# A hybrid layer in fp32 on one core: expert outputs are turned back during the last expert rounds, and the weight ring waits for the first gathered rows

## What is computed

```
def hier_moe(h2, ...):
    ...
    tok = zeros(n_rows).at[dest].set(flat_t[order])       # assignments sorted by expert
    ...
    def expert_block(args):
        xb, e = args
        hid = silu(xb @ w_gate_e[e]) * (xb @ w_up_e[e])
        return hid @ w_down_e[e]
    ys = lax.map(expert_block, (xs, block_e))
    return zeros_like(h2).at[tok].add(ys * wt[:, None])    # weighted sum back to the tokens

x = x + y_moe                                              # end of the first block
hn = rmsnorm([meta, x], a_norm_g);  qkv = hn @ a_w_qkv     # start of the second
```

## Time and profile before

| what | us |
|---|---|
| median of three runs | 2805.41 |
| lowest and highest run | 2804.01, 2805.78 |
| profiled execution, its own time | 2804.31 |
| its span from the first to the last instruction | 2802.5 |
| first ring load issued | 790.07 |
| gather 0 issued | 810.37 |
| first expert product starts | 823.41 |
| last "up" product starts | 1296.45 |
| last write of YSO ends | 1309.88 |
| first product of the combine | 1314.24 |
| first and second weights of the second block, first products | 1351.23 and 1360.02 |
| sums of the squares on PE | 1367.46 |

### The profile page before, as it was taken

The page is one execution under the profiler, slowest core; times in us unless marked ns, Lnnn a source line. Parts: engine busy times, 40 slices in busy tenths (PEclk is TensorE's granted clock), DMA queues, the critical chain, the costliest instruction groups (busy, mean ns, idle before and its releaser), DMA issues.

```text
span 2802.5 us, 41956 instructions
## 1 busy us (share of the span) xinstructions
PE 2608.5 (93%) x16786; PEld 2134.3 (76%) x16786; DVE 1150.9 (41%) x2012; ACT 1032.6 (37%) x2128; POOL 837.9 (30%) x532
## 2 busy tenths in 40 slices
PE   8999899999978888888999989999999999999999
PEld 6877788888855555455887769999998887777877
DVE  7754676231241111111356552232446776512212
ACT  4444444432222211112355544322324555532231
POOL 1002565223311223100221006645531110465553
PEclk9999999999989999999999989999999999999999
DMA  4330111433359999996211102323322111233332
GB/s 145 83 78 23 31 39 39 113 85 96 87 220 394 426 426 426 426 425 252 68 52 59 50 24 75 99 81 88 100 80 61 46 46 39 60 90 91 105 92 67
DMA packets 311731, 370.43 MB, mean 132 GB/s; under 512 B 10208, under 2 KB 283744, under 8 KB 286960
## 3 DMA queue, kind: packets, MB, share of 16 engines
q1 hardware_dynamic: 310384, 363.52, 37.2%
q0 software_dynamic: 1152, 4.19, 0.4%
HBM read 363.49 MB, written 4.19 MB: 131 GB/s over the span
## 4 chain that ended last, share of the span: by engine, by line
PE 67%; DMA 12%; DVE 9%; ACT 5%; POOL 3%; issue 3%; ACTq 0%; SPq 0%; DVEq 0%; POOLq 0%
DMA early<-in_w_up_e 11%; PE bank L2300 5%; PE bank L1823 5%; PE bank L2301 4%; PE bank L2302 4%; PE bank L2793 4%; PE bank L2794 4%; PE bank L2795 4%; PE bank L442 4%; PE bank L444 4%; PE bank L443 4%; POOL split L2275 2%; DVE early L683 2%; PE bank L3055 1%; PE bank L1060 1%
## 5 line engine op out<-in xcount | busy, mean ns | idle before, releaser
L2275 POOL TENSOR_TENSOR split<-keep,split 128x1024 fp32r<-128x1024 f32 x143 | 351.5, 2462 | 460.8 <-ACT split L2249 460.8
L2300 PE MATMUL bank<-x_hi,split 128*128 128x264 f32 (+1 forms) x1280 | 400.5, 313 | 21.9 <-POOL split L2275 9.4
L2301 PE MATMUL bank<-x_lo,split 128*128 128x264 f32 (+1 forms) x1280 | 392.7, 307 | 0.0
L2302 PE MATMUL bank<-x_hi,split 128*128 128x264 f32 (+1 forms) x1280 | 392.4, 307 | 0.0
L2249 ACT ACTIVATE split<-keep 128x1024 fp32r<-128x1024 f32 x192 | 200.2, 1049 | 222.1 <-PE bank L2795 208.0
L2300 PEld LDWEIGHTS bank<-x_hi,split 128*128 128x128 f32 x1280 | 243.7, 190 | 44.0 <-issue 20.8
L1823 PE MATMUL bank<-early 128*64 128x256 f32 x2048 | 236.0, 383 | 43.3 <-DMA early<-in_w_up_e 35.8
L1823 PEld LDWEIGHTS bank<-early 128*64 128x64 f32 x2048 | 166.4, 138 | 124.3 <-issue 79.3
L2301 PEld LDWEIGHTS bank<-x_lo,split 128*128 128x128 f32 x1280 | 244.0, 191 | 10.0 <-issue 0.2
L2302 PEld LDWEIGHTS bank<-x_hi,split 128*128 128x128 f32 x1280 | 242.8, 190 | 10.4
L2831 DVE TENSOR_TENSOR mlp<-mlp,bank 128x264 f32<-128x264 f32 (+1 forms) x96 | 49.5, 516 | 326.6 <-ACT mlp L2810 326.6
(11 more groups left out here) (476 smaller groups left out, 6089.5 us busy)
## 6 DMA issues: line engine op xcount, KB each, us to landing
early<-in_w_gate_e SPq DMA_DIRECT2D x64, 1024.0 KB, 11.1
early<-in_w_up_e SPq DMA_DIRECT2D x64, 1024.0 KB, 11.8
early<-in_w_down_e SPq DMA_DIRECT2D x64, 1024.0 KB, 11.3
early<-in_w_in SPq DMA_DIRECT2D x68, 512.0 KB, 3.7
keep<-in_mlp_w_in SPq DMA_DIRECT2D x64, 512.0 KB, 3.9
keep<-in_mlp_w_out SPq DMA_DIRECT2D x64, 512.0 KB, 3.9
keep<-in_a_w_qkv SPq DMA_DIRECT2D x24, 512.0 KB, 3.7
early<-in_w_ssd_out SPq DMA_DIRECT2D x16, 512.0 KB, 3.9
```

What stands on the lines that cost most here:

```text
L2275: e.tensor_tensor(lo, x, whole(hi), ALU.subtract).then_inc(*u.free(sig_, "lo", n))
L2300: e.matmul(o, hi[:, k, :], xh, start=k == 0, stop=False, skip_group_check=True)
L2301: e.matmul(o, hi[:, k, :], xl, start=False, stop=False, skip_group_check=True)
L2302: m = e.matmul(o, lo[:, k, :], xh, start=False, stop=k == 7, skip_group_check=True)
```

## The change

Five things are changed.

1. **Ring.** After the four stores of `h_rows`, SP waits until gather 0 has landed before it issues the next ring loads.
2. **Arrival.** ACT now copies the first bank of a gather, DVE the second.
3. **Window.** DVE reads both starts of a pair's window before it waits for the gathered rows.
4. **Rows turned back early.** "turn" s for s = 0 to 5 stands at the end of rounds 27 to 32, and "turn" 6 at the start of round 33. Each turns both halves of block s; ACT copies each bank once, with the weight, to YK, which lies over YSO. "half" 0 to 2 (rounds 27 to 29) and 3, 4 (round 33) make the upper and lower halves of q = 0 from YK in SBUF. YKL lies over YK too. Only block 7 is still turned in the combine.
5. **Combine.** PE starts with s = 0 to 4, turns block 7, and does s = 5 to 7. For tiles t = 4 to 7 the order is t outermost: one bank gets all eight blocks and is then done. PE and DVE no longer wait for the last write of YSO before they read the count. The function table load and the masks on ACT stand behind the halves. The third keep load of the second block waits for PE's s = 1.

The diff, cut (the wide path gets the same steps in its own branch, which is not taken):

```diff
-        def arrive_dve(e, n):
+        def arrive_act(e, n):
             b = BR.of("gather", n, 0)
             e.wait_ge(*GA.pe.to(n, 0))
...
+            if r == 33:
+                EXPERT += [("turn", 6), ("half", 3), ("half", 4)]
...
+            if 27 <= r < 33:
+                EXPERT.append(("turn", r - 27))
+            if 27 <= r < 30:
+                EXPERT.append(("half", r - 27))
...
                         e.dma_start(hrows[128 * c:128 * c + 128, :], HS[:, c, :]).then_inc(*d_rows.land(c))
+                    e.wait_ge(*d_got[0].to(0))
...
+        def return_pe(e, s_):
+            for q in range(2):
+                b = XR.take("yk", s_, q)
+                for s, n in b.before:
+                    e.wait_ge(s, n)
+                e.wait_ge(*F.act.to("y", 2 * (24 + s_) + 1, q))
+                for j in range(4):
+                    m = e.transpose(b.ap[:, cols(j, 128)], YSO[:, q * 4 + j, cols(s_, 128)], C["ident"])
...
+        def return_act(e, s_):
...
+                e.activation(rows_at(YK, q, s_), b.ap[:, :].rearrange("p (k n) -> p k n", n=128), ACT.Copy,
+                             scale=SWT[:, s_:s_ + 1]).then_inc(*b.free(B.act, "rows", s_, q))
+        def upper_act(e, q, s_):
...
+            e.activation(upper(q, s_), rows_at(YK, q, s_), ACT.Copy).then_inc(*B.act.up("hi", q, s_))
+        def lower_dve(e, q, s_):
+            e.wait_ge(*B.act.to("hi", q, s_))
+            e.tensor_tensor(rows_at(YKL, q, s_), rows_at(YK, q, s_), whole(upper(q, s_)), ALU.subtract)...
...
         def combine_pe(e):
+            bs = [BR.take("back", t) for t in range(4)]
+            for s_ in range(8):
+                if s_ == BEGUN:
+                    return_pe(e, 7)
...
+            for t in range(4, 8):
+                b = BR.take("back", t)
...
+                for s_ in range(8):
```

More of the change, by code:

```diff
@@ L1871, in expert_act @@
                     arrive_act(e, i)
+                if what == "turn":
+                    return_act(e, i)
+                if what == "half":
+                    upper_act(e, 0, i)
                 if what == "spread":
@@ L1905, in window_dve @@
             x = XWR.take(i)
+            if i == 0:
+                e.wait_ge(*E.dve.to("ints"))
+            ats = [window(e, 2 * i + j) for j in range(2)]
             if i < 8:
@@ L1912, in window_dve @@
                 e.wait_ge(s, n)
-            for j in range(2):
-                at = window(e, 2 * i + j)
+            for j, at in enumerate(ats):
                 m = e.tensor_copy(x.ap[:, :, cols(j, 64)], XSO[:, :, at])
@@ L1923, in expert_dve @@
                     arrive_dve(e, i)
+                if what == "half":
+                    lower_dve(e, 0, i)
                 if what == "meta":
@@ L1980, in build @@
                                              for n in ("weights", "x", "up", "silu", "hidden", "down", "y"))
+        f_t, f_r, f_i, f_l = (ctx.enter_context(nc.semaphore(f"wide_{n}")) for n in ("turned", "rows", "upper", "lower"))
         go = {n: ctx.enter_context(nc.semaphore(f"wide_go_{n}")) for n in ("pe", "dve", "act")}
@@ L2054, in wide_dve @@
                 begin(e, "dve")
+                for s_ in range(BEGUN):
+                    e.wait_ge(f_i, s_ + 1)
+                    e.tensor_tensor(rows_at(YKL, 0, s_), rows_at(YK, 0, s_), whole(upper(0, s_)), ALU.subtract).then_inc(f_l, 1)
         def wide_act(e):
@@ new lines, in combine_dve @@
+        def combine_dve(e):
+            for s_ in range(BEGUN, 7):
+                lower_dve(e, 0, s_)
+            for q in range(2):
+                b = XR.of("yk", 7, q)
+                e.wait_ge(*B.act.to("hi", q, 7))
+                e.scalar_tensor_tensor(out=rows_at(YKL, q, 7), in0=b.ap[:, :].rearrange("p (k n) -> p k n", n=128), scalar=SWT[:, 7:8],
+                                       in1=whole(upper(q, 7)), op0=ALU.mult, op1=ALU.subtract).then_inc(*b.free(B.dve, "lo", q, 7))
+            for s_ in range(7):
+                lower_dve(e, 1, s_)
+            for t in range(8):
+                b, r = BR.of("back", t), R[:, t, 16:T2]
+                e.wait_ge(*B.pe.to("back", t))
+                e.tensor_tensor(r, r, b.ap[:, :], ALU.add).then_inc(*b.free(B.dve, "x2", t))
+                if t == 3:
+                    for k in range(4):
+                        NA1.lo(e, k)
+                    split_lo(e, 2, True)
+                if t > 4:
+                    NA1.lo(e, t - 1)
@@ L2101, in combine_dve @@
             NA1.lo(e, 7)
[L2102 removed]
         def combine_act(e):
             e.wait_ge(*F.pe.to("oT", 31, 1))
+            for s_ in range(BEGUN, 7):
+                upper_act(e, 0, s_)
+            for q in range(2):
+                b = XR.of("yk", 7, q)
+                e.wait_ge(*B.pe.to("yk", 7, q))
+                e.activation(upper(q, 7), b.ap[:, :].rearrange("p (k n) -> p k n", n=128), ACT.Copy,
+                             scale=SWT[:, 7:8]).then_inc(*B.act.up("hi", q, 7))
```

136 lines of the change are left out of this document (72 added, 64 removed).

## The result

The changed kernel takes 2788.45 us (median of 6 runs, 2787.18 to 2790.97); the kernel before took 2804.27 us (6 runs, 2802.19 to 2805.78). The ratio is 0.9946, 95% interval 0.9935 to 0.9956. The forecast was 2788.6; it was worked out from three runs of the kernel before, with a median of 2805.41, so it stood for a gain of 16.8, and between the two medians here there are 15.8. The profiled execution of the changed kernel took 2788.55 us.

The account below looks back on a forecast made before the run. PE, busy 93% of the span, was taken as the main bound, with DMA bounding the expert rounds. 2804.3 - 3.8 (head) - 13.0 (tail) = 2787.5, plus 1.1 for the median of runs: 2788.6 us, range 2785 to 2795.

Parts of the forecast that it names:

- Head: From gather 0's issue through the first "up" to the expert rounds: 3.8 us sooner, bounds -1.2 and -4.5.
- The term for the arrival: Before the first "up": PE's extra wait of 1.18 us, for DVE's register reads after the gathered rows, goes.
- The jam at gathers 1 to 3: Rival: these gathers meet the held loads; at 17.2 us PE loses 8.4, time 2797; chance 0.15, shared with gather 0 no faster.
- Rounds 27 to 32: Expert rounds with added turns: 0.88 us of PE each, hidden under load waits, so no change in time.
- The cover of 1.7 us: PE's waits for loads in a round, 0.50 and 1.20 us, expected to hide 1.4 us of added work.
- Tail: From the start of the last "up" to the sums of the squares: -13.0 us, bounds -8 and -14.
- the start: From the last "up" to the combine's first product: 14.6 us instead of 17.8, so -3.2.
- the combine: 128 products, turn 7 and one wait of 1.0 us: 31.7 us against 35.5 before, so -3.8.
- the second block: Both products before the sums run through without waits: 11.7 us against 17.7, so -6.0.
- The lower clock: PE at 1.2 GHz again once or twice in the tail, 1.6 us each; counted only in the bound.
- The wait for bank 0: In the combine before tile 4, PE waits 1.0 us: 7.0 us of copies, lower half and add against 6.0 of PE work.
- Behind the sums: All steps after the sums of the squares shift along with them; 1435.04 us to the end of the span, unchanged.

## Why the prediction was right

**Head: right.** Gather 0 was put at 4.9 us and took 4.60; the head was put at -3.8, and -3.77 was measured at the first "up", -4.11 at the last. The 0.34 between them is inside the spread of the rounds. With the hold out, the landing is back at 7.35 and 2.9 us are lost. The term for the arrival, the copies and the register reads together, was sized too large, 1.2 for 0.88: the prediction let the whole wait go, and 0.30 of it stays. The first "up" was forecast for 819.6 and came at 818.80, since gather 0 itself was issued 0.84 us earlier, behind code that the change doesn't touch. Over all fourteen profiles that issue lies between 808.00 and 812.39, which a comparison of two spans takes in whole.

**The jam at gathers 1 to 3: the mechanism is there, the price isn't.** They did slow down, from 5.1 to 7.5 us at the median. The 8.8 us of room counted in the rival was enough. The Trainium skill (DMA: Bandwidth & Descriptors, Queues, rings and completion order) says that the engines take turns between queues; the 7.5 us between the 5.1 of empty engines and the 17.1 of the fullest agrees with that, but no run here shows the order of the packets.

**Rounds 27 to 32: right**, also that a loss begins where the cover ends. The cover of 1.7 us less 0.88 + 0.5 should leave 0.3, and 0.35 is left. On the way two errors met: PE's wait for DVE grew by 0.8 and not by 0.5 (1.39 against 0.59), and "out", which no longer waits for a copy, became 0.3 shorter. With 1.76 more, 1.4 a round lies over the cover, and the round became 1.0 longer: most of what lies over it is not hidden.

**Tail: the sum right, its terms off by more than a microsecond, in both directions.** Forecast were 3.2 for the start, 3.8 for the combine and 6.0 for the second block; measured are 4.4, 3.6 and 5.0, which makes 13.0 both times. That the errors cancel is luck. As times of the changed kernel, which the table has, the start is 1.2 us shorter than forecast, the combine 1.5 longer and the second block 0.3 shorter.

The prediction took the 1.52 us between ACT's last write and the first product as one price, of reading the count and branching, and kept it whole ahead of the combine. In fact 0.57 stands there. The records of PE's sequencer show why: in before it reads the count at 1309.92, behind the wait for ACT, and branches at 1310.87, in 0.36 us, with nothing under it; in the changed kernel it reads at 1303.50, under the last "out", and only what follows the read is left. So taking the wait for the last write of YSO away hid the read too. The combine's 1.31 us come seven products later, where the prediction had nothing. They are gone in the kernel without the other body, but the kernel before has the branch and no such wait, so this was not to be read from its trace.

The combine's own sum has two slips: 128 products of 0.23 us are 29.4 and not 29.8, and nine starts of 0.6 with 0.75 and 0.68 are 6.8 and not 7.0. The lower clock, which the prediction kept as a bound of the tail, didn't come in this trace; it came once with the turns in round 33.

The second block was forecast to run through in 11.7 us, and it does, in 11.43. Its gain was put at 6.0 because the prediction let it begin at 1349.7, where DVE adds the first of the tiles; PE's last product of the combine ends at 1351.06. The 1.3 us between them belong to the combine of before. And the reason given, that tile 4 is done long before tile 7, is only a part: by the order of the tiles alone it is 1.5 of the 5.0. The wait for weight 1's lower half and the lower clock behind it, which the prediction named too, are the likely source of 3 more.

**The wait for bank 0: right**, 1.0 forecast and 1.14 measured. Nine copies, one lower half and the add were put at 7.0 us; from ACT's first copy of turn 7 at 1316.32 to PE's next product at 1323.32 it is 7.00. The engine that sets the pace was another: the prediction counted ACT's copies, 0.6 apart, but they are 0.54 apart, and the chain follows DVE's lower halves, at 0.60. Had one cost the 0.75 that was assumed, seven would have taken 1 us more. The chain of waits of the changed kernel:

```profile
1318.45 4.21 DVE yk_lo L1844 x7
1322.66 0.61 DVE lasting L2175
```

Seven take 4.21 us, 0.60 each. The x halves became slower, a mean of 1326 ns against the 1051 of the earlier trace rows, at no cost: PE needs only the one of tile 7 late, and its products wait for none.

**Behind the sums: the assumption that failed.** Everything there was to shift along rigidly. It took 2.2 us more, 1437.25 against 1435.04. The code is the same. From 1690 to 2090 the two traces run in parallel, 18.9 us apart. Then come these stretches of before, first, and of the changed kernel, second (columns as in rows 6):

```profile
2109.00:2111.00 2.00, 2.00 (x8) 1.69 (x7) 1.66 (x3) 1.80 (x5) 0.00 (x0) 0.50 0.00 0
2111.00:2113.00 2.00, 2.00 (x18) 2.00 (x17) 1.67 (x5) 1.10 (x4) 0.00 (x0) 0.96 0.45 120
2113.00:2115.00 2.00, 2.00 (x19) 2.00 (x18) 1.69 (x2) 0.99 (x2) 0.00 (x0) 1.00 0.47 143
```

```profile
2090.00:2092.00 2.00, 2.00 (x8) 1.69 (x7) 1.66 (x3) 1.80 (x5) 0.00 (x0) 0.50 0.00 0
2092.00:2094.00 2.00, 2.00 (x11) 2.00 (x10) 1.68 (x5) 1.09 (x4) 0.00 (x0) 0.50 0.41 107
2094.00:2096.00 2.00, 2.00 (x13) 2.00 (x12) 1.70 (x2) 1.01 (x2) 0.00 (x0) 0.63 0.51 155
```

The first pair does the same work, product for product. Then before's clock is back at once, and the changed kernel's stays at 1.2 GHz for some 3 us more: 24 products in 4 us instead of 37, which at 0.11 us each is 1.4 us. From 2222 to 2226 there is a second such stretch, which before doesn't have, for some 1.7 us. What made the clock stay low was not found. Over all fourteen profiles this stage of identical code takes between 1432.9 and 1437.5 us, the most of it 1437.5 in a kernel whose tail is the changed one's and the least 1432.9 in another such, so the change isn't seen to be the cause. So the exact hit of the median is partly luck. What was forecast as 16.8 came out as 17.1; 0.84 us came on top from gather 0's earlier issue, and 2.2 were lost again behind; the profiled execution moved by 15.7.

## To carry to other kernels

A transfer that PE waits for can be made faster by holding back the transfers that nobody waits for yet, and here it was free, since the ring behind it was full anyway: ask which tile the next held load would have gone into. Work added to rounds that wait for loads was free here up to PE's remaining wait in those rounds, and mostly paid beyond it; read that wait first. A stage of unchanged code came back 2.2 us different here, and up to 4.5 between two profiles, so differences of that size are read from the stages, not from spans.

## What was not expected of the hardware

- Around a branch over a body that isn't run, PE stood 0.57 us at the jump (0.56 to 0.66 in eleven traces) and 1.31 us (0.95 to 1.48 in ten traces) after seven products that ran. In three other traces with the same branch the second wait is absent. With the read, the branch and the body gone from PE's program both are gone and the tail is 2.4 us shorter.
- A gather of 128 rows, 512 KB, landed after 4.3 to 4.6 us in eleven profiles in which the three loads, or two of them, were held back, after 7.0 to 7.5 behind three loads of 1 MB (three profiles), and after up to 17.2 when the loads' queue is full. One load of 1 MB ahead of it made no difference.
- The subtraction on DVE with two operands in SBUF took 0.60 us per 128x512 with POOL idle. One x half took 0.77 us with POOL idle and three in a row 1.5 us each with POOL at work. Another took 0.76 with POOL at work too, at 1338.76, so POOL being busy does not always slow it:

```profile
1324.97 4.50 DVE L2422 SCALAR_TENSOR_TENSOR x_lo<-lasting,x_hi 128x528 fp32r<-128x528 f32 x3
1334.98 0.77 DVE L2422 SCALAR_TENSOR_TENSOR x_lo<-lasting,x_hi 128x528 fp32r<-128x528 f32 x1 [0.28 <-ACT x_hi L2405]
1338.76 0.76 DVE L2422 SCALAR_TENSOR_TENSOR x_lo<-lasting,x_hi 128x528 fp32r<-128x528 f32 x1
```
